# Squares of the recurrent stages' norms in a step of their own, earlier in the program and in the buffer of the inverse root; the mLSTM's denominators divided by thirds

## The reference

```python
# GDN: q and k are normalised over the 128 elements of a head, after convolution and SiLU
q = l2_norm(q) * (GDN_HEAD_DIM ** -0.5)
k = l2_norm(k)
...
o = chunk_gated_delta_rule(q, k, v, g, beta)
o = rms_norm(o, w_norm) * silu(z)            # the "out" norm of GDN, then @ w_out
...
# mLSTM
den = s_inter * (q . n_vec) + sum(w_intra)
h_c = num / max(abs(den), exp(-m_row))       # the division by denominators
hs = rms_norm(hs, w_norm) * sigmoid(o)       # the "mout" norm, then @ w_out
```

## Time and profile before

| | |
|---|---|
| median of three runs | 4295.78 us |
| the profiled execution's own time | 4293.81 us |
| its span | 4291.9 us |
| mean granted TensorE clock | 0.942 |
| TensorE matmul busy | 3921.9 us, 91% |
| VectorE busy | 2567.2 us, 60% |
| ScalarE busy | 1553.1 us, 36% |
| GpSimd busy | 758.1 us, 18% |

### The profile page before, as it was taken

The page is one execution under the profiler, slowest core; times in us unless marked ns, Lnnn a source line. Parts: engine busy times, 40 slices in busy tenths (PEclk is TensorE's granted clock), DMA queues, the critical chain, the costliest instruction groups (busy, mean ns, idle before and its releaser), DMA issues.

```text
span 4291.9 us, 62567 instructions
## 1 busy us (share of the span) xinstructions
PE 3921.9 (91%) x25559; PEld 3622.3 (84%) x25559; DVE 2567.2 (60%) x5015; ACT 1553.1 (36%) x2769; POOL 758.1 (18%) x613
## 2 busy tenths in 40 slices
PE   7999989889979999998999999999889999978999
PEld 5667869789969999896888888888789998977999
DVE  4654328899959999997455555555452433555342
ACT  4544223345533333333433323332342424444231
POOL 0000005466722332331111110111000001110000
PEclk9999999999989999998789999999889998988999
DMA  3112324358879999994001101010022211112222
GB/s 112 56 61 68 98 69 139 126 177 282 269 236 323 334 332 327 320 331 155 26 26 35 35 30 40 30 35 26 30 85 88 89 64 50 60 40 69 87 92 69
DMA packets 203069, 528.19 MB, mean 123 GB/s; under 512 B 17032, under 2 KB 91272, under 8 KB 202784
## 3 DMA queue, kind: packets, MB, share of 16 engines
q1 hardware_dynamic: 99792, 341.22, 23.8%
q0 software_dynamic: 37440, 136.33, 9.1%
q10 hardware_dynamic: 65552, 46.64, 3.5%
HBM read 477.99 MB, written 46.14 MB: 122 GB/s over the span
## 4 chain that ended last, share of the span: by engine, by line
PE 65%; DVE 23%; ACT 6%; issue 4%; DMA 1%; POOL 0%; DVEq 0%; ACTq 0%; POOLq 0%; SPq 0%
PE bank L94 64%; DVE wl L121 4%; DVE acc L131 3%; DVE H L121 2%; ACT wh L115 2%; DVE row L163 2%; DVE yc L131 1%; DVE eq L121 1%; PE bank L97 1%; DMA raw<-in_v 1%; DVE aal L121 1%; DVE fs L121 1%; DVE sq L131 1%; ACT Xh L115 1%; DVE Xl L121 1%
## 5 line engine op out<-in xcount | busy, mean ns | idle before, releaser
L94 PE MATMUL bank<-Xh,wh 128*128 128x272 f32 (+3 forms) x3680 | 1244.9, 338 | 60.8 <-ACT ft L115 25.5
L94 PE MATMUL bank<-Xl,wh 128*128 128x272 f32 (+3 forms) x3680 | 1173.2, 319 | 0.0
L94 PE MATMUL bank<-Xh,wl 128*128 128x272 f32 (+3 forms) x3680 | 1170.7, 318 | 0.0
L121 DVE TENSOR_TENSOR wl<-raw,wh 128x1024 fp32r<-128x1024 f32 (+1 forms) x536 | 576.1, 1093 | 477.7 <-ACT wh L115 476.5
L115 ACT ACTIVATE wh<-raw 128x1024 fp32r<-128x1024 f32 (+1 forms) x632 | 589.1, 953 | 703.2 <-PE bank L94 660.5
L94 PEld LDWEIGHTS bank<-Xh,wh 128*128 128x128 f32 x3680 | 719.3, 195 | 132.4 <-issue 66.0
L94 PEld LDWEIGHTS bank<-Xl,wh 128*128 128x128 f32 x3680 | 720.8, 196 | 18.6 <-issue 2.4
L94 PEld LDWEIGHTS bank<-Xh,wl 128*128 128x128 f32 x3680 | 717.8, 195 | 20.8
L121 DVE TENSOR_TENSOR H<-H,bank 128x384 f32<-128x384 f32 (+3 forms) x522 | 252.4, 490 | 353.6 <-PE bank L94 350.0
L94 PE MATMUL bank<-aah,wh 128*128 128x384 f32 x1024 | 356.4, 348 | 43.3 <-DVE wl L121 23.5
L121 POOL TENSOR_TENSOR wl<-raw,wh 128x1024 fp32r<-128x1024 f32 x96 | 273.6, 2852 | 517.2 <-ACT wh L115 516.9
(11 more groups left out here) (305 smaller groups left out, 6469.8 us busy)
## 6 DMA issues: line engine op xcount, KB each, us to landing
raw<-in_u SPq DMA_DIRECT2D x128, 512.0 KB, 4.0
raw<-in_v SPq DMA_DIRECT2D x128, 512.0 KB, 5.9
raw<-in_up SPq DMA_DIRECT2D x64, 512.0 KB, 3.6
raw<-in_down SPq DMA_DIRECT2D x64, 512.0 KB, 3.5
scratch<-gb ACTq DMA_DIRECT2D x12, 2048.0 KB, 13.8
gj<-scratch SPq DMA_DIRECT2D x32, 768.0 KB, 7.3
raw<-in_w_gdn SPq DMA_DIRECT2D x48, 512.0 KB, 3.5
raw<-in_w_att SPq DMA_DIRECT2D x36, 512.0 KB, 3.5
```

Source lines behind the costliest of these rows:

```text
L94: return Issued(self, self.q and self.q.matmul(out, l, r, start=start, stop=stop), 1)
L121: return Issued(self, self.q and self.q.tensor_tensor(out, a, b, op), 1)
```

## The change

- A new step `rms_squares` squares on ScalarE straight into the buffer that will hold the inverse root (`rt`, `ro`), and a new step `rms_total` does the one product by ones on TensorE. The ring SQ is no longer used by these norms.
- q and k: the squares follow SiLU at once (dense step 8 after the projection), the sum is at step 12 instead of 10, the inverse root at 14 instead of 12, the scaling at 16 instead of 14.
- Out norms: the squares of thirds 0 and 1 are put into the scan, after its chunks 3 and 6, one stage before their sums. Those of third 2 stay in the output part, behind the gating of third 0, whose buffer they take; so ScalarE now waits there for VectorE's gating.
- mLSTM: `ml_div` waits only for its own third of the denominators. Thirds 0 and 1 are divided (and then squared) after chunks 3 and 6 of the chain; only third 2 is divided in the output part, whose weight in `merge` falls from 13 to 10.
- GpSimd's product by the gate is a step of its own, `times_z`, at the same place.

```diff
+        def squares_ahead(key, buf, before, x, scale, *needs):
+            RT.at[key], RT.before[key] = buf, before
+            RMS[key] = (PA, [x], x.shape[-1] if len(x.shape) == 2 else 384, scale, needs)
+            do("rms_squares", key)
+
+        def sums_now(key):
+            PA.take(key)
+            PA.give(key, ("ln",) + key)
+            do("rms_total", key)
...
-                                after(8, lambda p=p, n=n: do("conv_qk", p, n))
-                                after(10, lambda p=p, n=n: l2_sums(p, n))
-                                after(12, lambda p=p, n=n: [do("rms_inv", ("l2", p, n, hf)) for hf in range(2)])
-                                after(14, lambda p=p, n=n: l2_scale(p, n))
+                                after(8, lambda p=p, n=n: l2_squares(p, n))
+                                after(12, lambda p=p, n=n: [sums_now(("l2", p, n, hf)) for hf in range(2)])
+                                after(14, lambda p=p, n=n: [do("rms_inv", ("l2", p, n, hf)) for hf in range(2)])
+                                after(16, lambda p=p, n=n: l2_scale(p, n))
...
+        def out_squares(p, g):
+            key = ("out", p, g)
+            RO.take(key)
+            squares_ahead(key, RO.at[key], RO.before[key], three(flat_pair(VD.at[p]), g), 1.0 / 128, ("o", p, 3 * g + 2))
...
-            sums(0)
-            sums(1)
+            sums_now(("out", p, 0))
+            sums_now(("out", p, 1))
             yield 1
-            do("rms_inv", ("out", p, 0))
-            do("rms_inv", ("out", p, 1))
+            inverse(0)
+            inverse(1)
             yield 2
             gate(0)
+            out_squares(p, 2)
             yield 1
-            sums(2)
             gate(1)
+            sums_now(("out", p, 2))
             yield 1
-            do("rms_inv", ("out", p, 2))
+            inverse(2)
...
@@ scan_gdn, after each chunk
+                if c in (3, 6):
+                    out_squares(p, c // 3 - 1)
...
+        def divided(p, g):
+            do("ml_div", p, g)
+            if g < 2:
+                ml_squares(p, g)
...
@@ out_ml
-            for g in range(3):
-                do("ml_div", p, g)
-                yield 1
-            DEN1.give(p, ("mnum", p, 2))
-            sums(0)
-            sums(1)
+            divided(p, 2)
+            sums_now(("mout", p, 0))
+            sums_now(("mout", p, 1))
...
@@ chain_ml, after each chunk
+                if c in (3, 6):
+                    divided(p, c // 3 - 1)
...
-                streams.append((chains(t), 13 * (t > 1) + 26 * (t < 5)))
+                streams.append((chains(t), 10 * (t > 1) + 26 * (t < 5)))
...
-                dv.wait_ge("mden", p, 8)
+                dv.wait_ge("mden", p, 3 * g + 2)
...
+            def rms_squares(key):
+                _, (x,), n, scale, needs = RMS[key]
+                r = clear(ac, RT, key)[:, 0:n]
+                for signal in needs:
+                    ac.wait_ge(*signal)
+                ac.act(r, x, ACT.Square, scale=math.sqrt(scale)).then_inc("sq", *key, 0)
```

More of the change, by code:

```diff
@@ L1208, in after, with l2_squares @@
                 later.sort(key=lambda x: x[0])
-            def l2_sums(p, n):
+            def l2_squares(p, n):
+                do("conv_qk", p, n)
                 RT.take((p, n))
                 for hf, (a, b) in enumerate(HALVES):
[L1213 to L1220, removed]
+                    squares_ahead(("l2", p, n, hf), RT.at[p, n][:, a:b], RT.before[p, n], YC.at[p, n][:, a:b], 1.0,
+                                  ("silu", p, n))
             def l2_scale(p, n):
@@ L1352, in levels_gdn, with inverse @@
                     yield 1
+        def out_squares(p, g):
+            key = ("out", p, g)
+            RO.take(key)
+            squares_ahead(key, RO.at[key], RO.before[key], three(flat_pair(VD.at[p]), g), 1.0 / 128, ("o", p, 3 * g + 2))
         def out_gdn(p):
[L1355 to L1364, removed]
+            def inverse(g):
+                do("rms_inv", ("out", p, g))
+                do("times_z", ("out", p, g))
             def gate(g):
@@ L1558, in dense_ml, with ml_squares, inverse @@
                 OX1.give(p, ("dense", g))
-        def out_ml(p):
[L1561 to L1570, removed]
+        def divided(p, g):
+            do("ml_div", p, g)
+            if g < 2:
+                ml_squares(p, g)
+        def ml_squares(p, g):
+            key = ("mout", p, g)
+            RO1.take(key)
+            squares_ahead(key, RO1.at[key], RO1.before[key], three(flat_pair(VD1.at[p]), g), 1.0 / 128, ("mnum", p, g))
+        def out_ml(p):
+            def inverse(g):
+                do("rms_inv", ("mout", p, g))
+                do("times_z", ("mout", p, g))
             def gate(g):
@@ L1574, in gate @@
                 RO1.give(("mout", p, g), ("mog", p, g, 1))
-            for g in range(3):
-                do("ml_div", p, g)
-                yield 1
-            DEN1.give(p, ("mnum", p, 2))
-            sums(0)
-            sums(1)
-            yield 1
-            do("rms_inv", ("mout", p, 0))
-            do("rms_inv", ("mout", p, 1))
+            divided(p, 2)
+            sums_now(("mout", p, 0))
+            sums_now(("mout", p, 1))
+            yield 1
+            inverse(0)
+            inverse(1)
+            DEN1.give(p, ("mnum", p, 2))
             yield 2
             gate(0)
+            ml_squares(p, 2)
             yield 1
-            sums(2)
             gate(1)
+            sums_now(("mout", p, 2))
             yield 1
-            do("rms_inv", ("mout", p, 2))
+            inverse(2)
             yield 2
@@ L1718, in rms_sum, with rms_total @@
                         "ssum", *key, i)
+            def rms_total(key):
+                ps = PS[clear(pe, PA, key)][:, 0:RMS[key][2]]
+                pe.wait_ge("sq", *key, 0)
+                pe.mm(ps, ONES, RT.at[key][:, 0:RMS[key][2]]).then_inc("ssum", *key, 0)
             def rms_part(key, i, need):
@@ L2000, in pe_program @@
             program(pe, dict(
-                fence=fence, constants=constants, dense=dense, rms_sum=rms_sum, rms_part=rms_part, att_vt=att_vt, scores=scores, transp=transp,
+                fence=fence, constants=constants, dense=dense, rms_sum=rms_sum, rms_total=rms_total, rms_part=rms_part, att_vt=att_vt, scores=scores, transp=transp,
                 values=values, key_scores=key_scores, weights=weights, x_rows=x_rows, row_sums=row_sums,
@@ L2887, in ac_program @@
             program(ac, dict(
-                fence=fence, constants=constants, split=split, rms_sum=rms_sum, rms_part=rms_part, rms_inv=rms_inv, norm=norm, x_load=x_load, meta_in=meta_in, lam=lam, att_copy=att_copy,
+                fence=fence, constants=constants, split=split, rms_sum=rms_sum, rms_squares=rms_squares, rms_part=rms_part, rms_inv=rms_inv, norm=norm, x_load=x_load, meta_in=meta_in, lam=lam, att_copy=att_copy,
                 att_vt=att_vt, exps=exps, transp=transp, att_out=att_out, att_split=att_split, gate=gate,
@@ L2992, in keys_out, with times_z @@
                 po.tt(three(tb, g), b3(IDENT), three(tb, g), ALU.subtract).then_inc("tb0", p, g)
-            def rms_inv(key):
-                if key[0] not in ("out", "mout"):
-                    return
+            def times_z(key):
                 _, p, g = key
@@ L3041, in po_program @@
                 fence=fence, constants=constants, split=split, att_bias=att_bias, row=row,
-                gdn_dup=gdn_dup, gdn_zero=gdn_zero, keys_twice=keys_twice, decay=decay, pair_kq=pair_kq, keys_out=keys_out, rms_inv=rms_inv,
+                gdn_dup=gdn_dup, gdn_zero=gdn_zero, keys_twice=keys_twice, decay=decay, pair_kq=pair_kq, keys_out=keys_out, times_z=times_z,
                 ml_dup=ml_dup, ml_zero=ml_zero, ml_decay=ml_decay))
```

## The result

The changed kernel takes 4224.98 us, the median of four runs from 4216.41 to 4243.35; the kernel before, on the same chip, 4298.08 us. The ratio is 0.9836 with a 95% interval of 0.9814 to 0.9858. Run a second time beside other kernels it gave 4230.42 us and 0.985 (0.9828 to 0.9871). The forecast was 4230 us.

What follows compares the result with a forecast made beforehand. TensorE, busy 91% of the span, was taken to bound the kernel by its work plus idle time. Terms summing to -66.1 us took 4293.81 to 4227.7, forecast 4230 us allowing for the median; own range 4214 to 4246, overall 4207 to 4270.

Steps and rivals of the forecast that it cites:

- A: GDN out norms, stages 3 to 7: TensorE's wait before the pair of sums goes, -15.7 us.
- C: GDN out norms, stages 8 to 10: shorter waits at the sums, 2.0 in stage 8, 0.8 each in 9 and 10, -3.6 us.
- D: GDN q and k norms: most of the sums' 14.4 us wait goes, less 0.8 for a delayed scan copy, -10.4 us.
- F: mLSTM output parts, stages 2 and 3: waits before sums of thirds 0 and 1 go, 10.5, plus clock 4.6, -15.1 us.
- G: mLSTM output part, stage 4: waits of 8.4 us shrink to 1.6 at the third sum, -6.8 us.
- H: mLSTM stage 5: one division instead of three, so the third sum comes at 3852.6 instead of 3858.45, -5.8 us.
- I: mLSTM: cost of moved divisions holding VectorE, 0.9 us at each of four places in stages 2 and 3, +3.5 us.
- B: GDN stages 3 to 7: half-clock windows behind the pair's wait go, five of 1.7 us, -8.5 us.
- E: GDN stages 3 to 7: half clock behind the q sum's wait partly goes, somewhat under half of 5 x 1.7, -3.7 us.
- The held ScalarE: GDN stages: third 2's square waits for third 0's gating, holding ScalarE 3.1 us a stage; cost to TensorE 0.
- The held queue: Rival, both layers: holds of ScalarE and VectorE pass to TensorE in full with half clock, 94 us, giving 4320; chance 0.06.
- Waits only move: Rival, both layers: sums stop waiting but the next instruction needing ScalarE or VectorE waits as long, about 4292; chance 0.06.

Runs made afterwards that it cites:

- e9_after: The changed kernel run a second time, beside other kernels: 4230.4 us, 0.9850 of the kernel before.
- e5_filler: Kernel before plus 14 dummy 128x128 products in front of third 0's out-norm sum in each of GDN stages 3 to 7: 4266.1 us, 0.9931.
- e2_qk: Kernel before with only the q and k norm part of the change: 4301.9 us, 1.0017.
- e1_gdn_out: Kernel before with only the GDN out norm part of the change: 4251.9 us, 0.9913.
- e4b_divend: Changed kernel with third squares in a spare buffer, mLSTM squares of thirds 0 and 1 one chunk later, last division at the output part's end: 4223.4 us.
- e6_thirds: Kernel before with only the mLSTM divisions by thirds, squares and sums where they were: 4281.2 us, 0.9963.
- e7_conv: Changed kernel with the GDN v slab convolutions three dense steps later: 4184.6 us, 0.9743 of the kernel before.
- e12_conv_all: Changed kernel with v slab convolutions three dense steps later and q and k convolutions four later: 4204.1 us, 0.9793 of the kernel before.

## Why the prediction was right, and where its parts were not

The time came out: 4225 and 4230 for 4230. Two errors cancelled in it. The terms for waiting (A, C, D, F, G and H less I, with F's waits as 10.5) came to 49.3 us; TensorE's idle time fell by 33.6 and 35.1. The terms for the clock (B, E, F's 4.6) came to 16.8 us; by the means the half-clock loss fell by 34 to 40, and busy time (mean span less idle) by some 34.

The profiles tell where. The mLSTM from 3600 us of before, ahead of the first output part, to the last third sum, before and after, the same 1727 matmuls:

```profile
3600.01:3858.45 258.44, 227.37 (x1727) 214.20 (x1725) 133.46 (x210) 111.56 (x254) 30.32 (x39) 0.92 0.16 52
```

```profile
3568.92:3809.29 240.37, 218.68 (x1727) 209.67 (x1725) 133.04 (x212) 110.25 (x254) 29.98 (x40) 0.97 0.18 56
```

They are 18.1 us shorter (19.6 in e9_after), where F, G, H and I make 24.2. Idle time fell by 9.4 us, of a forecast 19.6, and busy time by 8.7 us (10.2 in e9_after), of a forecast 4.6. GDN stages 3 to 7 are 22.0 us shorter in the profile after (613.10 us) and 26.8 in e9_after, where A, B, E and the 8.4 us of q and k waits there make 36.3. Their busy time fell by 1.9 and 6.6 us, of a forecast 12.2 for B and E. So the waiting came out smaller than forecast in both layers, and the clock gave more in the mLSTM and, by these two profiles, less in stages 3 to 7.

- **A, -15.7.** Right: no wait at the pair in stages 3 to 7, and none came in its place there.
- **B, -8.5, and E, -3.7.** The direction was right, the size was not to be had from the windows behind the waits. The windows named went to 1.00, but the stretches behind `rc`, which I had left out of the sum, grew: up to 17 us each. e5_filler, which fills term B's five waits, is 29 us faster as a whole and 8.4 us faster in those stages in its one profile; so B's size is open between the two. E, added as a separate term, was wrong: the q and k part alone raises the loss by 23 us.
- **C, -3.6.** The third sums of stages 9 and 10 wait 6.10 and 5.92 us, not 4 to 5; net the waits of the 384 wide form outside stages 3 to 7 fell from 14.8 (30.5 - 15.7) to 12.0, and 0.8 us for `dd` is new in stage 8: -2.0.
- **D, -10.4.** At the sums it held: 14.4 to 3.5 us. But 3.9 us for `ke` are new. In stage 2 the waits before the scan's products (1.75 for `rt` and 0.46 for `xr`) became one of 2.04 for `xr`, 0.2 less. So -7.2. I had written that the later scaling is far from its use. It is, but not from its neighbours: VectorE in GDN stage 3 after the change, with the new wait:

```profile
2327.27 0.77 DVE L131 SCALAR_TENSOR_TENSOR q<-yc,rt 128x16 f32<-128x16 f32 x2
2327.96 0.49 DVE L127 TENSOR_SCALAR yc<-xc,cols 128x528 f32<-128x528 f32 x1
2328.48 2.38 DVE L131 SCALAR_TENSOR_TENSOR yc<-xc,cols,yc 128x528 f32<-128x528 f32 x3
2330.78 0.55 DVE L121 TENSOR_TENSOR ke<-bank,lc 128x384 f32<-128x384 f32 x1
```

```profile
2331.38 0.49 PE L94 MATMUL bank<-vn,ke 64*128 64x128 f32 x4 [0.78 <-DVE ke L121]
```

  The scaling of q takes 0.77 us directly ahead of the convolution of k and `ke`, and TensorE waits 0.78. e2_qk has the same 3.8 us, and e1_gdn_out has none.
- **F, -15.1.** Waits 10.5 became 1.1 + 1.9 at the third sums, which I had covered with 16 dense steps: -7.5. The square waits for division and gating both. Of the clock part the direction held: the window behind the pair of stage 2 (3604.70 us) is at 1.00, and the mLSTM's parts together won more than these 4.6 us.
- **G, -6.8.** 8.4 became 4.26: -4.1. I forecast a wait of 1.6.
- **H, -5.8.** From the chain's last product to the third sum it was 15.5 us before (3842.93 to 3858.45) and is 11.3 now: -4.2. The product before, and both after:

```profile
3842.93 0.39 PE L94 MATMUL bank<-dd,ones 128*128 128x128 f32 x2
```

```profile
3797.98 0.39 PE L94 MATMUL bank<-dd,ones 128*128 128x128 f32 x2
...
3809.29 1.62 PE L94 MATMUL bank<-ro,ones 128*128 128x384 f32 x2 [8.14 <-ACT ro L115]
```

  The step that failed is the sentence that splits and banks have slack in stages 1 and 4. ScalarE and VectorE around the start of stage 5, after:

```profile
3799.66 0.52 ACT L115 ACTIVATE ro<-vd 128x384 f32<-128x384 f32 x1 [3.82 <-DVE vd L121]
...
3800.72 2.02 ACT L115 ACTIVATE wh<-raw 128x1024 fp32r<-128x1024 f32 x2
```

```profile
3796.48 2.55 DVE L135 RECIPROCAL den<-den 128x384 f32<-128x384 f32 x1
...
3801.83 2.36 DVE L121 TENSOR_TENSOR wl<-raw,wh 128x1024 fp32r<-128x1024 f32 x2 [1.52 <-ACT wh L115]
3804.10 0.35 DVE L127 TENSOR_SCALAR den<-den 128x384 f32<-128x384 f32 x1
```

  The division of third 1 comes at the very end of the chain; ScalarE stands 3.82 us for it, the weights are split behind it, and the last division waits for the splits.
- **I, +3.5.** `H` waits are 4.0 us where 0.9 stood, in stages 2 to 4: 1.33 + 0.34 twice and 0.6. Good to 0.4 us. But 1.7 us for the mLSTM's `dd`, once in stage 4, are new as well, and no term holds them.
- **The held ScalarE, 0.** Right: 3.11 us against a forecast 3.1 and no wait behind it. VectorE's second `bb` did wait about 1 us for it, not 0.1, without TensorE noticing.
- **The range.** Redone from the two bounds that it names, it is 4221 us (E at 8.5, I at 0) to 4257 (clock terms at nothing, I at 14), and not 4214 to 4246. What was measured lies in both.

The rivals: VectorE did not take the 41.9 us of A to E back, only the 3.9 us of D above. The held queue did not pass its waits on. "Waits only move" is wrong for the whole and right in two places: e4b_divend's stage 10, and the half-clock stretches.

Left open: what sets a stretch's length. Stretches of 3.4 and of 27 us stand behind waits of the same 2.60 us, before the same product, in the kernel before and in e6_thirds. The same kernel's runs differ in it as well: the changed kernel ran in 4216.41 us at a mean clock of 0.953 and in 4243.35 at 0.947, 0.006 of 4230 being 25 of the 27 us. e5_filler shows for five places of one kind that the wait causes half clock, e7_conv only that it goes with `rc`'s wait: there the convolution was moved, not the wait filled.

## What to carry to other kernels

Price a wait of some 3 us of a nearly always busy TensorE at more than its length: filling five such waits with useless products made this kernel 29 us faster, though no wait was shortened. It is no rule for every wait: ten of up to 2.0 us left the granted clock at 0.99 in e12_conv_all. Terms for waiting may be added, terms for the clock may not: the three parts' clock losses sum to -14 us and the whole has -34 to -40, and one edit cost 7 us alone but did not in company. So after each step look at which wait is now the longest in the stage and what clock stands behind it. And when a step moves two places later, read what its instructions now stand directly in front of (a scaling of 0.77 us became a wait of 0.78), and where a moved division falls at the end of a stage, whether the next stage's weight splits queue behind it.

## What the runs showed of the hardware

- The granted clock drops to 0.50 behind TensorE's waits of 2.2 to 3.3 us and stays there from 3.4 to 27 us, while TensorE works without a gap (27.20 of 27.20 us busy at 0.50 in e2_qk, 27.30 of 27.30 in e6_thirds). The same code has 3.4 us there in one profile and 27.3 in another.
- Adding 70 products of 128x128 in place of waiting raised the mean granted clock from 0.942 to 0.948 and made the kernel 29 us faster.
- A reciprocal of 128x384 f32 on VectorE took 2.55 us, a TENSOR_SCALAR of that size 0.35 (stage 5's start after).
- The loading of a table takes 1.28 us with an exponential 0.01 us behind its end (2417.77 + 1.28 to 2419.06). This bears out the reading of the earlier trace rows. The Trainium skill (ScalarE: Activation LUTs, What ACT_TABLE_LOAD costs) adds a drain of 1.38 us to the load; none shows here.
